# Attention values by feature on two halves of TensorE's columns, scores in two banks' parts, and low parts of weights on GpSimd

## What is computed

```python
hx = modulate(rms_norm_2(x, norm1_g[l]), ...)        # x: 512 tokens of 1024
zx = jnp.split(hx @ w_in[l], 10, axis=-1)            # ten parts of 256
a_val, a_gate, q, k, v, u, sv, bg, cg, xin = zx
# four heads; keys and values of 256 context tokens stand ahead of the 512
p1 = softmax(q1 @ k1.T * scale); p2 = softmax(q2 @ k2.T * scale)
y_b = rms_norm_2((p1 - lam * p2) @ v, subln_g) * (1.0 - lam_init)
y_a = silu(layer_norm(depthwise_conv(a_val * sigmoid(a_gate), 31 taps)))
y_c = gelu(u) * (mix of 128 x 128 by group, of layer_norm(gelu(sv)))
y_d = bg * depthwise_conv(cg * xin, 3 taps)
x = x + ... * (concatenate([y_a, y_b, y_c, y_d]) @ w_out[l])
x = x + ... * channel_mixer(...)                      # 1024 -> 4096 -> 1024
```

## Time and profile before

| | |
|---|---|
| time, median of 3 runs | 2116.89 us (2112.39 to 2120.92) |
| the profiled execution's own time | 2115.37 us |
| its span | 2113.5 us |
| mean granted clock of TensorE | 0.998 |
| TensorE busy | 2040.2 us |
| DVE, ACT, GpSimd busy | 1270.3, 795.1, 72.4 us |

### The profile page before, as it was taken

One profiled execution on the slowest core, in us unless ns is written; L12 is line 12 of the kernel. 1 busy time (PEld: TensorE's weight loads), 2 busy tenths in 40 slices (PEclk: granted clock), 3 DMA queues, 4 the chain that ended last, 5 costly groups with the idle time before them and its releaser, 6 DMA issues.

```text
span 2113.5 us, 26503 instructions
## 1 busy us (share of the span) xinstructions
PE 2040.2 (97%) x11156; PEld 1739.0 (82%) x11156; DVE 1270.3 (60%) x1696; ACT 795.1 (38%) x1117; POOL 72.4 (3%) x81
## 2 busy tenths in 40 slices
PE   6999999999999999999999999999998999999998
PEld 5989888778788888887888888888787787888887
DVE  7466866867657885727546455464689645344343
ACT  4333334584343455534113122132536534132231
POOL 0000000000120000020000000001100010000001
PEclk9999999999999999999999999999999999999999
DMA  8643523525322531222333232232353122232221
GB/s 290 224 159 120 213 86 129 186 90 188 131 100 74 162 92 70 70 82 98 111 111 120 90 120 100 100 122 105 112 167 90 70 90 89 91 100 100 100 95 65
DMA packets 54054, 249.18 MB, mean 118 GB/s; under 512 B 6224, under 2 KB 12512, under 8 KB 35504
## 3 DMA queue, kind: packets, MB, share of 16 engines
q1 hardware_dynamic: 52048, 242.41, 33.4%
q10 hardware_dynamic: 1296, 2.63, 0.3%
q0 software_dynamic: 592, 2.46, 0.3%
HBM read 232.53 MB, written 12.06 MB: 116 GB/s over the span
## 4 chain that ended last, share of the span: by engine, by line
PE 85%; DVE 9%; ACT 3%; issue 2%; DMA 1%; POOL 0%; ACTq 0%; DVEq 0%; POOLq 0%
PE banks L1957 70%; DVE small L1351 2%; PE banks L1981 1%; PE banks L1982 1%; PE banks L1983 1%; PE banks L652 1%; PE banks L531 1%; ACT whi_f L2107 1%; PE banks L643 1%; DVE wlo_f L2317 1%; DVE ntx L2351 1%; PE banks L607 1%; PE banks L606 1%; PE banks L608 1%; PE banks L2013 1%
## 5 line engine op out<-in xcount | busy, mean ns | idle before, releaser
L1957 PE MATMUL banks<-hxh,whi_f 128*128 128x512 f32 (+1 forms) x1464 | 585.4, 400 | 24.3 <-ACT hxh L2136 7.5
L1957 PE MATMUL banks<-hxh,wlo_f 128*128 128x512 f32 (+1 forms) x1464 | 569.7, 389 | 0.0
L1957 PE MATMUL banks<-hxl,whi_f 128*128 128x512 f32 (+1 forms) x1464 | 555.2, 388 | 0.2 <-DVE hxl L2386 0.2
L2317 DVE TENSOR_TENSOR wlo_f<-raw_f,whi_f 128x2048 fp32r<-128x2048 f32 x133 | 304.9, 2293 | 181.4 <-ACT whi_f L2107 181.2
L2107 ACT ACTIVATE whi_f<-raw_f 128x2048 fp32r<-128x2048 f32 x133 | 253.7, 1907 | 308.3 <-PE banks L1957 290.1
L1957 PEld LDWEIGHTS banks<-hxh,whi_f 128*128 128x128 f32 x1464 | 276.1, 189 | 86.6 <-issue 27.5
L1957 PEld LDWEIGHTS banks<-hxh,wlo_f 128*128 128x128 f32 x1464 | 275.8, 188 | 57.9
L1957 PEld LDWEIGHTS banks<-hxl,whi_f 128*128 128x128 f32 x1464 | 274.9, 188 | 58.0 <-issue 1.9
L1957 PE MATMUL banks<-fxh,whi_f 128*128 128x512 f32 (+1 forms) x528 | 205.6, 389 | 2.1 <-DVE cT L1495 1.1
L1957 PE MATMUL banks<-fxh,wlo_f 128*128 128x512 f32 (+1 forms) x528 | 204.2, 387 | 0.0
L1957 PE MATMUL banks<-fxl,whi_f 128*128 128x512 f32 (+1 forms) x528 | 203.5, 385 | 0.0
(11 more groups left out here) (340 smaller groups left out, 3129.3 us busy)
## 6 DMA issues: line engine op xcount, KB each, us to landing
raw_f<-in_wst SPq DMA_DIRECT2D x133, 1024.0 KB, 4.9
mvr<-in_mst SPq DMA_DIRECT2D x120, 512.0 KB, 5.8
stack<-qk_parts SPq DMA_DIRECT2D x36, 192.0 KB, 6.6
x_kept<-xT SPq DMA_DIRECT2D x2, 2048.0 KB, 8.6
raw_f<-in_wst SPq DMA_DIRECT2D x8, 384.0 KB, 5.9
xT<-x_kept SPq DMA_DIRECT2D x2, 1536.0 KB, 8.7
qk_parts<-qk_h SPq DMA_DIRECT2D x3, 768.0 KB, 3.8
qk_parts<-qk_l SPq DMA_DIRECT2D x3, 768.0 KB, 3.6
```

The lines of the kernel that those rows point to most:

```text
L1957: last = pe.matmul(o, (wh, wl)[w][:, k, c, :], r[part][:, k, :], start=(k == order[0] and parts is not LOW and (w, part) == (0, 0)), stop= ...
L2317: dve.tensor_tensor(wlo[r][:], raw[r][:], whi[n % 2 if n > N_FIRST else n][:].bitcast(F32), ALU.subtract).then_inc(w_lo, 1)
```

## The change

There are six parts in it.

**Values by feature.** The product of probabilities and values takes the values as the stationary side (64 columns) and the turned probabilities as the moving one (128), and puts the even blocks of keys on one half of the output's rows and the odd ones on the other (L689). ACT copies this to `parts_sb` (`kept`), and a second product with a constant `adder` (two stacked unit matrices) adds the halves and turns them (`summed`, L704) into `vals`. `summed` stands at the step of start + 5, directly ahead of the next unit's turning. In layer 1 the values stand a step earlier, behind the scores.

**Own banks in layer 1.** The scores of the two softmaxes lie in bank parts of their own, each with its own count of scores, maxima and exponentials. DVE reduces each by itself.

**The wait for `onat`** moves from ahead of the six turnings to ahead of the fifth, and values waits for it too.

**Mixing of the gates** takes its two halves in turn. Its steps, and those of the means and spreads, are one later.

**Low parts on GpSimd.** Chunks `base + 6` to `base + 9` of each layer have their low parts made by GpSimd (`weights_low`). DVE does two taps of the convolution per unit instead of three in layer 1, and in layer 0 three in the first three units and two in the others, and more of them ahead of the units.

**High parts later.** ACT makes a high part no longer right behind the copy that ends a chunk, but at the end of the unit.

```diff
-        self.mean, self.sums, self.spread, self.mix = (53, 56, 58, 61) if l == 0 else (44, 49, 53, 57)
+        self.mean, self.sums, self.spread, self.mix = (54, 57, 59, 62) if l == 0 else (45, 50, 54, 58)
     def values(self, v):
-        return self.start(v) + 4
+        return self.start(v) + (4 if self.per == 5 else 3)
+
+    def summed(self, v):
+        return self.start(v) + 5
...
             def turn(v):
                 pe.wait_ge(q_w, u0 + v + 1)
                 pe.wait_ge(q_pt, u0 + v)
-                pe.wait_ge(q_on, u0 + v)
...
                 for b in range(6 if v % p.per < 4 else 4):
+                    if b == 4:
+                        pe.wait_ge(q_on, u0 + v)
...
                     for b in range(6):
-                        last = pe.matmul(vals[:, 0:64], ptd[:, v % 2, b * P:(b + 1) * P], vnat[:, b, hd],
-                                         start=(b == 0), stop=(b == 5))
+                        half = 64 * (b % 2)
+                        last = pe.matmul(by_feature[half:half + 64, :], vnat[:, b, hd], ptd[:, v % 2, b * P:(b + 1) * P],
+                                         start=(b < 2), stop=(b > 3))
...
+            def summed(v):
+
+
+                pe.wait_ge(at_out, 16 + u0 + v + 1)
+                for e in range(1 if v % p.per < 4 else 2):
+                    last = pe.matmul(vals[:, 64 * e:64 * e + 64], parts_sb[:, e * P:(e + 1) * P], adder[:], start=True, stop=True)
                 last.then_inc(q_o, 1)
...
                 for c in (1, 0):
-                    for g in (2 * c, 2 * c + 1):
-                        half = 64 * (g % 2)
-                        for j in range(nj):
+                    for j in range(nj):
+                        for g in (2 * c, 2 * c + 1):
+                            half = 64 * (g % 2)
...
+            def kept(v):
+
+
+                upto(p.values(v))
+                act.wait_ge(at_o, 16 + u0 + v + 1)
+                if v:
+                    act.wait_ge(q_o, u0 + v)
+                src, w = (by_feature, P) if v % p.per < 4 else (turned[:, T:T + 2 * P], 2 * P)
+                act.activation(parts_sb[:, 0:w], src, ACT.Copy).then_inc(at_out, 1)
...
                 for v in range(v0, v1):
+                    if v > v0:
+                        kept(v - 1)
                     if v + 1 < v1:
                         exp(v + 1, 0)
...
             y_high(2)
             y_high(3)
             if two:
+                kept(last)
                 scaled(last)
...
+                if l:
+                    for i, s in enumerate(score_parts):
+                        dve.wait_ge(q_s, p.counted(v, i))
+                        dve.tensor_reduce(dnm[:, z + i:z + i + 1], s, AX_X, ALU.max, negate=True).then_inc(q_m, 1)
+                    return
...
-                    splits = due[0] is not None
-                    weights_due()
                     if v0 == 0:
-                        conv(0 if splits else 3)
+                        conv(3 if v < more else 2)
...
+            def weights_low(n):
+
+
+                pool.wait_ge(w_lo, n - N_FIRST)
+                pool.wait_ge(w_hi, n + 1 - N_FIRST)
+                pool.tensor_tensor(wlo[w_place(n)][:], raw[w_place(n)][:], whi[n % 2][:].bitcast(F32), ALU.subtract
+                                   ).then_inc(w_lo, 1)
...
                 pool.wait_ge(roped, 4 * l + 4)
                 pool.dma_start(wsT[:], sgw[l]).then_inc(ld_sg, 16)
                 pool.dma_start(bsg[:], sgb[l]).then_inc(ld_sg, 16)
+                for n in range(C_L + l * N_L + 6, C_L + l * N_L + N_WIN):
+                    weights_low(n)
```

More of the change, by code:

```diff
@@ L336, in build, with places @@
         score = flat[:, 2560:4096]
+        score_parts = [flat[:, 1024:1792], flat[:, 2048:2816]]
         y_att = [flat[:, 2048 + 1024 * c:2048 + 1024 * c + TX] for c in range(2)]
+        def places(l):
+            if l == 0:
+                return [acc[:, c, 0:T] for c in range(2)], score, turned, vals, flat[:, 2432:2560]
+            return [banks[:, c, :] for c in range(2)], flat[:, 1024:2816], flat[:, 3072:3840], flat[:, 3840:3968], flat[:, 3968:4096]
         mv_ps = aux[:, 1:3, :].rearrange("p a b -> p (a b)")
@@ L586, in layer @@
             u0 = p.u0
+            half_of, score, turned, vals, by_feature = places(l)
             def rotated(b, n):
@@ L711, in fill @@
                         scores(v)
+                for v in range(p.units):
                     if g == p.values(v):
                         values(v)
+                for v in range(p.units):
+                    if g == p.summed(v):
+                        summed(v)
                     if g == p.turned(v):
@@ L770, in layer @@
                             pe.wait_ge(ctx_out, j - 5)
-                        last = step(n, j % 2, k, c, own, order, lambda r: ctx_acc[:, c, :] if r[2] else acc[:, c, 0:T])
+                        last = step(n, j % 2, k, c, own, order, lambda r: ctx_acc[:, c, :] if r[2] else half_of[c])
                         if tail and i < 4:
@@ L941, in evict, with weights_due @@
                         act.activation(dst[:, :, oc:oc + TC], ctx_acc, ACT.Copy).then_inc(ctx_out, 1)
-                    act.activation(dst[:, c, o:o + T], acc[:, c, 0:T], ACT.Copy).then_inc(acc_free[c], 1)
+                    act.activation(dst[:, c, o:o + T], half_of[c], ACT.Copy).then_inc(acc_free[c], 1)
                 if c and j < 9:
-                    split(n + 2)
+                    weights_due()
+                    due[0] = n + 2
+            due = [None]
+            def weights_due():
+                if due[0] is not None:
+                    split(due[0])
+                due[0] = None
             done = [0]
@@ L956, in exp @@
                 upto(p.scores(v))
+                if part == 0 or p.parts == 2:
+                    act.wait_ge(q_m, p.counted(v, part))
                 if part == 0:
-                    act.wait_ge(q_m, u0 + v + 1)
                     if v >= 2:
@@ L970, in exp @@
                                              bias=dnm[:, z + o:z + o + 1], accum_out=dls[:, z + o:z + o + 1])
-                if part:
+                if part or p.parts == 2:
                     ins.then_inc(q_e, 1)
+            def kept(v):
+                upto(p.values(v))
+                act.wait_ge(at_o, 16 + u0 + v + 1)
+                if v:
+                    act.wait_ge(q_o, u0 + v)
+                src, w = (by_feature, P) if v % p.per < 4 else (turned[:, T:T + 2 * P], 2 * P)
+                act.activation(parts_sb[:, 0:w], src, ACT.Copy).then_inc(at_out, 1)
             def scaled(v):
-                upto(p.values(v))
+                upto(p.summed(v))
                 h, j, z = v // p.per, v % p.per, 4 * (v % 2)
@@ L1016, in run @@
                         out(v)
+                    weights_due()
             run(0, p.cut)
+            kept(p.cut - 1)
             scaled(p.cut - 1)
@@ L1210, in layer_dve @@
             u0 = p.u0
+            half_of, score, turned, _, _ = places(l)
             for o, w in ((0, 15), (T + 15, 30), (TX + 45, 15))[:3 if two else 2]:
@@ L1717, in bring_back @@
                 p = PLAN[l]
-                sync.wait_ge(q_s, p.u0 + p.per * (3 + part))
+                sync.wait_ge(q_s, p.counted(p.per * (3 + part) - 1))
                 k = slice(6, KT) if part else slice(0, 6)
```

65 lines of the change are left out of this document (40 added, 25 removed).

## The result

The changed kernel takes 2123.36 us (median of 16 runs, 2119.21 to 2130.93), the kernel before 2119.11 us beside it; the ratio over all their runs is 1.0026, with an interval from 1.0015 to 1.0037. The profiled execution took 2121.76 us. So it is slower by about a quarter of a per cent, where the forecast said 2120.

What follows compares the result with a forecast made beforehand. TensorE, busy 97%, was taken as the bound, with a loop of exponential, combine and reduction in layer 1. Layer 1 -2.2 and layer 0 +5.4 made +3.2 us, so 2120 against the median 2116.89; range 2107 to 2132.

Steps and rivals of the forecast that it cites:

- Part 5: GpSimd's low parts, 4.6 us each, hold DVE's taps and combine: +7.6 us in layer 1, +4.6 in layer 0.
- My choice: DVE's reductions, reading the banks, run on beside GpSimd; if held too, up to 1.8 us in four units, +7 at most.
- rival C: TensorE's clock falls to half behind stalls, 1.5 us each: 2128 to 2135 if two or more stalls exceed 2 us; chance 0.2.
- Part 1: Layer 1's steady unit, values by feature and their sum: 5.41 to 5.0 us, -0.41 in eight units, -3.3.
- Part 2: Other waits of layer 1: run starts -2.4 and -2.0, uneven units -1.5, ACT's later high part +1.3 us.
- The four uneven units: Units of layer 1's first run outside the steady ones: -1.5 us together.
- Part 3: Mixing of the gates with halves in turn: 4.29 to 2.9 us in layer 0, 2.57 to 1.9 in layer 1.
- Part 4: Layer 0 without holds: first run +1.1, gate's copy -0.6, mixing -1.3, tail about +1.65; together +0.8 us.
- The -0.6: Layer 0, second copy of the gate's values: no high part right behind it any more, -0.6 us.
- Part 6: Layer 1, ACT's high part behind `out` and ahead of `kept`: two places at 0.65, +1.3 us.
- Rival D: Values on the two halves don't run side by side, body stays 1.25 us: 2136; chance 0.05.
- rival B: GpSimd hardly holds DVE up, or waits for it: 2109 us, down to 2104; chance 0.27.

Runs made afterwards that it cites:

- lows_dve_by_token: Changed kernel with low parts back on DVE, high parts made at once and values by token again; 2112.0 us, ratio 0.9959 to the kernel before.
- low_pieces: Changed kernel with each GpSimd low part cut into eight instructions of 256 columns; 2112.8 us, ratio 0.9964 to the kernel before.
- lows_dve: Changed kernel with low parts back on DVE, high parts made at once and taps as before; 2118.5 us, ratio 0.9994 to the kernel before.
- only_lows: Kernel before with only the low parts on GpSimd, the later high parts and the new numbers of taps; 2134.8 us, ratio 1.0071.
- only_pieces: Kernel before with only GpSimd low parts in eight instructions each, the later high parts and the new numbers of taps; 2124.2 us, ratio 1.0017.

## Why the forecast held, and where its steps did not

**The number** was right, 2120 against 2123.4, and inside the range of 2107 to 2132. The kernel before itself, 2116.89 in the three runs that the forecast stood on, came to 2119.1 over more runs; as a change it is 3.1 forecast and 4.2 by the medians or 5.1 by the means. The sum behind it was right in part.

**Part 5, the holds**, is shown. That the one that comes second stands until the first is done was the step all rested on; each low part took 4.58 to 4.60, as worked out (4.6). The price of a hold was about 2.5 and 2.6 in layer 0, forecast 2.6 and 2.0: the offset of the scores' starts against before rises by 4.2 and 4.3 until the stretch at half clock is over, of which 1.7 each is clock. In layer 1 the second cost 2.5, forecast 3.3 (two units take 14.30 from scores to scores where lows_dve_by_token takes 10.13, less 1.7 of clock), the third 1.7, forecast 3.0 (TensorE's wait for it at 1651.29, with no such wait in low_pieces), and the first 0.6, forecast 1.3: there DVE's factor was held and took 1.34 for 0.22, and TensorE's turning behind it stood for 0.63. Together 9.9 for 12.2. The size in layer 1 is what was off: DVE's combine came 3.5 late, as worked out (3.2), but TensorE didn't pay all of it, and where it found the slack was not looked into. My choice that the reductions run on was right: they keep 1.81 beside GpSimd, wholly inside its stretch in low_pieces. This is also what the Trainium skill says of `tensor_reduce` (page SBUF — State Buffer, section Who interferes with whom), and the traces agree.

**The clock was left out of the sum** and put to rival C. That is the step that failed: by the estimate from the mean clocks 7.5 us are lost by it on top of what the kernel before loses, more than the 5.1 that the change costs. C's mechanism, a wait and then half clock, is in the trace at 756, 797 and 1620, at 1.7 each where C had 1.5. Its point of decision, two or more stalls over 2 us, was reached by my own sum, which had four of 2 to 3.3: some of it should have been in the sum. But C doesn't explain the 7.5 alone. Cutting the low parts gave back 3.8 by the clock (5.3 on top of the kernel before); putting them back on DVE gave back only 1.3, and there taking back values by feature gave another 4.4. And a wait alone doesn't decide it: behind 2.52 us in lows_dve the clock stayed. What I had not seen either is that the kernel before has the same thing by chance in other places, so that its one stretch in the profile was luck. That the number came out is owed to two errors of opposite sign, which is luck too: the sum at full clock was +3.2, measured about -2.4; the clock 0, measured +7.5.

**Part 1.** The body (0.86 forecast, 0.81 measured) and the sum (0.22; 0.17 to the turning) are right. Wrong is what they were subtracted from, "5.41 - 0.43 = 4.98 of TensorE's own": the idle time of 0.43 counts from the shown end of the product before, which is 0.40 long, while the next one starts 0.23 behind it when nothing is waited for. So 0.17 more of the gap was waiting. By token and with halves of the scores the unit comes to 4.80 with TensorE never waiting, so there was 4.80 and not 4.98 to begin with, and the sum, the wait of 0.2 for `onat` and the gap took what was gained. The steady unit did shrink, by 0.6 and not 0.41, but by part 2: `onat` stood behind the first exponential, and that started earlier by halves.

**Part 2.** 4.4 for the starts of the two runs: in lows_dve_by_token the scores' starts come closer by 1.6 and 0.4 at the first run and by 1.8 and 1.0 at the second, 4.8. Right. The four uneven units come closer by 2.4 in the changed kernel, 1.5 forecast.

**Part 3.** 2.9 and 1.9 forecast, 2.84 and 1.97 measured, right by itself; its worth in the whole isn't shown.

**Part 4.** The tail: 1.65 forecast, 5.50 - 3.78 = 1.7 measured. Right. The -0.6 at the gate's second copy did not come: TensorE's waits for the copies there (`svn`, `ug`, `cx`) are 5.3 us before and 5.8 after.

**Part 6**, the later high parts (1.3 in the sum), was never run alone; its share stays open. What a high part ahead of `onat` costs beside the new wait shows in lows_dve: a wait of 2.52 us.

**Rival D** is refuted by the body of 0.81, **rival B** by the taps of 5.27 and 6.00 and by only_lows with only_pieces.

## What to carry to other kernels

That nobody waits for work given to GpSimd doesn't make it free for DVE: look at what DVE does beside it with two inputs in SBUF, put reductions of the banks there, or cut GpSimd's instruction into short ones. When a change adds long waits to a TensorE-bound kernel, put a price on stretches at half clock in the sum (1.7 us each here), with a chance, and compare mean clocks of many runs, not one profile. An experiment that takes one part back can bring a wait of its own, as lows_dve did: look for it before its time is read as the part's worth. A product made shorter is worth nothing where the sum and the wait that it needs take as much again (4.79 against 4.80 us a unit here); try such parts one at a time.

## What the runs showed of the hardware

A hold lasts to the other's end whatever the held instruction's size: one column stood for 2.19 us, while a reciprocal with one input (0.17) and reductions of the banks (1.81) ran on. And the pace of TensorE varies at a granted clock of 1.00. In the same stretch of the same products, 1060:1440, without a wait, the kernel before and low_pieces show:

```profile
1060.00:1440.00 380.00, 379.46 (x2159) 329.17 (x2158) 197.85 (x270) 82.89 (x94) 0.00 (x0) 1.00 0.31 108
...
1060.00:1440.00 380.00, 379.46 (x2181) 332.27 (x2180) 202.19 (x275) 82.91 (x94) 0.00 (x0) 1.00 0.32 112
```

2159 and 2181 products in 380 us, 1% apart, which is nearly 4 us. The kernel before showed 2168 in its other profile. It is not a matter of records that a trace lacks: from one of ACT's high parts to the 22nd behind it, 1052.8 to 1426.5 and 1057.8 to 1427.3, it is 373.7 and 369.5 us. No cause for this was tried; it is why offsets outside the changed stretches say nothing here.
